# A hybrid decoder trunk in split fp32r products: the first layer's scores as three fp32r products of split queries and keys, and its attention two steps later

## The reference

```
for i in range(DEPTH):                       # DEPTH = 2, x is (1, 256, 2048) float32
    h = rmsnorm(x, g[0])
    y = swa_sink_attention(...) if i == 0 else forgetting_attention(...)
    x = x + rmsnorm(y, g[1]);  h = rmsnorm(x, g[2])
    x = x + rmsnorm((silu(h @ w_gate) * (h @ w_up)) @ w_down, g[3])

swa_sink_attention (32 query heads of 64, 8 key heads, blocks of 128 queries):
    qkv = h @ w_in;  q, k = partial_rotary(q), partial_rotary(k)
    s = einsum('bnqkgd,bnskd->bnkgqs', q, kband) * 64**-0.5, masked to a window of 128
    m = max(max(s), sink);  p = exp(s - m);  probs = p / (sum(p) + exp(sink - m))
    out = (probs @ vband) @ w_out
```

## Time and profile before

| | |
|---|---|
| median of 3 runs | 2123.86 us (2123.24 to 2123.88) |
| profiled execution, its own time | 2122.76 us |
| its span, first to last instruction | 2120.7 us |
| granted TensorE clock, mean | 0.999 of full speed |
| PE / DVE / ACT busy | 99% / 75% / 55% |

### The profile page before, as it was taken

One profiled execution on the slowest core, in us unless ns is written; L12 is line 12 of the kernel. 1 busy time (PEld: TensorE's weight loads), 2 busy tenths in 40 slices (PEclk: granted clock), 3 DMA queues, 4 the chain that ended last, 5 costly groups with the idle time before them and its releaser, 6 DMA issues.

```text
span 2120.7 us, 32295 instructions
## 1 busy us (share of the span) xinstructions
PE 2108.9 (99%) x9723; PEld 1727.9 (81%) x9723; DVE 1598.4 (75%) x3267; ACT 1165.7 (55%) x2093; POOL 151.5 (7%) x291
## 2 busy tenths in 40 slices
PE   9999999999999999999999999999999999999998
PEld 7877888888888888888778777888888888888886
DVE  6777577876678876778888888578776678776786
ACT  7767565544545444555656556565454555445453
POOL 2111000000000000000152241000000000000000
PEclk9999999999999999999999999999999999999999
DMA  7544856565665656665687786656655665656652
GB/s 262 188 140 134 213 180 216 190 188 177 201 214 186 195 171 199 198 199 163 185 249 212 216 234 201 201 191 201 196 180 178 198 217 188 188 177 201 214 188 90
DMA packets 208957, 409.29 MB, mean 193 GB/s; under 512 B 14208, under 2 KB 15392, under 8 KB 208368
## 3 DMA queue, kind: packets, MB, share of 16 engines
q1 hardware_dynamic: 203008, 389.86, 58.8%
q0 software_dynamic: 5584, 18.16, 3.1%
q10 hardware_dynamic: 288, 0.33, 0.0%
HBM read 401.44 MB, written 6.85 MB: 193 GB/s over the span
## 4 chain that ended last, share of the span: by engine, by line
PE 50%; DVE 1%; issue 1%; ACT 0%; POOLq 0%; POOL 0%; DVEq 0%
PE bank L1309 16%; PE bank L1310 16%; PE bank L1311 16%; PE bank L1395 1%; PE bank L1358 1%; DVE ring_lo L786 0%; DVE k_t L846 0%; DVE q_t L857 0%; PE bank L1322 0%; PE bank L1369 0%; ACT y_sb L599 0%; PE bank L1341 0%; POOLq L157 0%; POOL post_r L1168 0%; DVE x_sb L1137 0%
## 5 line engine op out<-in xcount | busy, mean ns | idle before, releaser
L1309 PE MATMUL bank<-ring_hi,a_hi 128*128 128x512 f32 x2240 | 883.1, 394 | 1.0 <-DVE ring_lo L786 1.0
L1311 PE MATMUL bank<-ring_hi,a_lo 128*128 128x512 f32 x2240 | 872.7, 390 | 0.0
L1310 PE MATMUL bank<-ring_lo,a_hi 128*128 128x512 f32 x2240 | 872.4, 389 | 0.0
L586 ACT ACTIVATE ring_hi<-stage,g_t 128x512 fp32r<-128x512 f32 x992 | 661.5, 717 | 363.0 <-DMA stage<-ffn_w_gate_up 207.6
L786 DVE SCALAR_TENSOR_TENSOR ring_lo<-stage,g_t,ring_hi 128x512 fp32r<-128x512 f32 x992 | 707.7, 757 | 162.4 <-ACT ring_hi L586 160.4
L1309 PEld LDWEIGHTS bank<-ring_hi,a_hi 128*128 128x128 f32 x2240 | 420.6, 188 | 91.9 <-issue 5.9
L1311 PEld LDWEIGHTS bank<-ring_hi,a_lo 128*128 128x128 f32 x2240 | 420.5, 188 | 88.8
L1310 PEld LDWEIGHTS bank<-ring_lo,a_hi 128*128 128x128 f32 x2240 | 421.0, 188 | 83.6
L784 DVE TENSOR_TENSOR ring_lo<-stage,ring_hi 128x512 fp32r<-128x512 f32 x480 | 306.9, 690 | 138.1 <-ACT ring_hi L584 136.9
L584 ACT ACTIVATE ring_hi<-stage 128x512 fp32r<-128x512 f32 x480 | 277.8, 624 | 178.3 <-PE bank L1311 154.1
L1309 PE MATMUL bank<-ring_hi,h_hi 128*128 128x512 f32 x704 | 274.4, 390 | 0.0
(11 more groups left out here) (150 smaller groups left out, 861.3 us busy)
## 6 DMA issues: line engine op xcount, KB each, us to landing
stage<-ffn_w_gate_up SPq DMA_DIRECT2D x352, 512.0 KB, 4.6
stage<-ffn_w_down SPq DMA_DIRECT2D x176, 512.0 KB, 5.6
stage<-fox_w_in SPq DMA_DIRECT2D x96, 512.0 KB, 5.0
stage<-swa_w_in SPq DMA_DIRECT2D x48, 512.0 KB, 4.5
stage<-swa_w_out SPq DMA_DIRECT2D x64, 256.0 KB, 4.1
stage<-fox_w_out SPq DMA_DIRECT2D x32, 512.0 KB, 4.8
p_scratch<-p_blocks POOLq DMA_DIRECT2D x12, 384.0 KB, 4.8
p_f<-p_scratch POOLq DMA_DIRECT2D x48, 96.0 KB, 4.6
```

The source lines that it names most:

```text
L586: nc.scalar.activation(ring_hi[:, n % RING, :], src, ACT.Identity, scale=g_t[:, row * KT + j:row * KT + j + 1]).then_inc(hi_ready, 1)
L1309: nc.tensor.matmul(dst, hi_a, hi_w, start=start, stop=False)
L1310: nc.tensor.matmul(dst, hi_a, lo_w, start=False, stop=False)
L1311: return nc.tensor.matmul(dst, lo_a, hi_w, start=False, stop=stop)
```

## The change

The transposed queries and keys of the first layer are split. ACT writes the high part (`high_transposed`, semaphore `qk_high`), DVE then the rest in place of its copy, and only that gives the bank back (`tr_read`). The scores are three fp32r products. All keys of `STD` and `LAST` grow by 2, as do `QK_ATTENDED` (22 to 24) and two entries of `LATE_O`. The second layer is as it was.

```diff
-STD = dict(scores={6: (0, 1), 22: (2, 3)},
-           turned={14: 0, 16: 1, 18: 2, 20: 3, 30: 4, 31: 5, 33: 6, 35: 7},
+STD = dict(scores={8: (0, 1), 24: (2, 3)},
+           turned={16: 0, 18: 1, 20: 2, 22: 3, 32: 4, 33: 5, 35: 6, 37: 7},
...
-QK_ATTENDED = 22
+QK_ATTENDED = 24
...
+            def high_transposed(u, t):
+                act.wait_ge(tr_done, TR[("qk", u, t)] + 1)
+                dst = k_hi if u == 0 else q_hi
+                nc.scalar.activation(dst[:, :, tok(t)], turn_bank(u, t)[:, :].rearrange("p (k m) -> p k m", k=GH // 2),
+                                     ACT.Identity).then_inc(qk_high, 1)
...
             def read_transposed(u, i, t):
-                dve.wait_ge(tr_done, n + 1 + TR_LOOP * i)
-                dst = k_t if u == 0 else q_t
-                nc.vector.tensor_copy(dst[:, :, tok(t)], turn_bank(u, t)[:, :].rearrange("p (k m) -> p k m", k=GH // 2)).then_inc(tr_read, 1)
+                if u < U_FOX:
+                    dve.wait_ge(qk_high, n + 1)
+                    hi, lo = (k_hi, k_lo) if u == 0 else (q_hi, q_lo)
+                    nc.vector.tensor_tensor(lo[:, :, tok(t)], src, hi[:, :, tok(t)].bitcast(F32), ALU.subtract).then_inc(tr_read, 1)
...
                 for lo, hi, keys in ((0, P, P), (P, SEQ, SEQ)):
                     for a in range(2):
+                        if G < NG:
+                            nc.tensor.matmul(dst, q_hi[rows, m, lo:hi], k_hi[rows, b, 0:keys], start=True, stop=False)
...
+                    if G < NG:
+                        for q, k in ((q_hi, k_lo), (q_lo, k_hi)):
+                            for a in range(2):
+                                last = nc.tensor.matmul(score_bank(G, 2 * m + a)[:, lo:lo + keys], q[rows, m, lo:hi], k[rows, b, 0:keys],
+                                                        start=False, stop=k is k_hi)
```

More of the change, by code:

```diff
@@ L54 @@
 U_END = U_FFN[1] + 3 * FG
-STD = dict(scores={6: (0, 1), 22: (2, 3)},
-           maxima={6: (0, 1), 8: (2, 3), 22: (4, 5), 24: (6, 7)},
-           exps={7: 0, 8: 1, 10: 2, 11: 3, 23: 4, 24: 5, 26: 6, 27: 7},
-           scaled={9: 0, 13: 1, 25: 2, 29: 3},
-           turned={14: 0, 16: 1, 18: 2, 20: 3, 30: 4, 31: 5, 33: 6, 35: 7},
[L66 to L72, removed]
+STD = dict(scores={8: (0, 1), 24: (2, 3)},
+           maxima={8: (0, 1), 10: (2, 3), 24: (4, 5), 26: (6, 7)},
+           exps={9: 0, 10: 1, 12: 2, 13: 3, 25: 4, 26: 5, 28: 6, 29: 7},
+           scaled={11: 0, 15: 1, 27: 2, 31: 3},
+           turned={16: 0, 18: 1, 20: 2, 22: 3, 32: 4, 33: 5, 35: 6, 37: 7},
+           pv={24: (0, 1), 40: (2, 3)}, out={25: 0, 41: 1})
+LAST = dict(scores={8: (0, 1), 26: (2,), 33: (3,)},
+            maxima={8: (0, 1), 10: (2, 3), 26: (4, 5), 33: (6, 7)},
+            exps={9: 0, 10: 1, 12: 2, 13: 3, 27: 4, 28: 5, 34: 6, 35: 7},
+            scaled={12: 0, 16: 1, 30: 2, 37: 3},
+            turned={17: 0, 19: 1, 21: 2, 23: 3, 33: 4, 35: 5, 40: 6, 42: 7},
+            pv={26: (0, 1), 45: (2, 3)}, out={})
 FOX = dict(scores={14: (0, 1), 34: (2, 3)},
@@ L114 @@
 LATE_O = {0: [(0, 1)], 2: [(1, 1)], 4: [(2, 1)], 8: [(3, 1)], 10: [(4, 1)], 12: [(5, 0), (5, 1)],
-          26: [(6, 0), (6, 1)], 44: [(7, 0), (7, 1)]}
+          28: [(6, 0), (6, 1)], 46: [(7, 0), (7, 1)]}
 LATE_O_FOX = {0: [(0, 1)], 2: [(1, 1)], 4: [(2, 1)], 6: [(3, 1)], 8: [(4, 1)], 10: [(5, 0), (5, 1)],
@@ L209, in build @@
         q_t = at("q_t", 28 * KB, [P, GH // 2, SEQ])
+        k_hi = at("k_hi", 24 * KB, [P, GH // 2, SEQ], F32R)
+        q_hi = at("q_hi", 28 * KB, [P, GH // 2, SEQ], F32R)
+        k_lo = at("k_lo", 12 * KB, [P, GH // 2, SEQ], F32R)
+        q_lo = at("q_lo", 45 * KB, [P, GH // 2, SEQ], F32R)
         prob = at("prob", 32 * KB, [P, 4, 3 * P + NT])
@@ L252, in build @@
         tr_done, tr_read, qk_turned = sem("tr_done"), sem("tr_read"), sem("qk_turned")
+        qk_high = sem("qk_high")
         scored, row_maxed, maxed, exped = sem("scored"), sem("row_maxed"), sem("maxed"), sem("exped")
@@ L699, in unit @@
                             forget_gate(s + STEPS * (u - U_FOX))
+                        if u < U_FOX:
+                            for v, t in qk_copied(u, s):
+                                high_transposed(v, t)
                     for G, when, at_step in groups(u, s):
@@ L834, in read_transposed @@
                 n = TR[("qk", u, t)]
-                dve.wait_ge(tr_done, n + 1 + TR_LOOP * i)
-                dst = k_t if u == 0 else q_t
-                nc.vector.tensor_copy(dst[:, :, tok(t)], turn_bank(u, t)[:, :].rearrange("p (k m) -> p k m", k=GH // 2)).then_inc(tr_read, 1)
+                src = turn_bank(u, t)[:, :].rearrange("p (k m) -> p k m", k=GH // 2)
+                if u < U_FOX:
+                    dve.wait_ge(qk_high, n + 1)
+                    hi, lo = (k_hi, k_lo) if u == 0 else (q_hi, q_lo)
+                    nc.vector.tensor_tensor(lo[:, :, tok(t)], src, hi[:, :, tok(t)].bitcast(F32), ALU.subtract).then_inc(tr_read, 1)
+                else:
+                    dve.wait_ge(tr_done, n + 1 + TR_LOOP * i)
+                    nc.vector.tensor_copy(q_t[:, :, tok(t)], src).then_inc(tr_read, 1)
             def turn_keys(u, i, a):
@@ L1357, in scores @@
                         rows = slice(DH * a, DH * (a + 1))
-                        last = nc.tensor.matmul(score_bank(G, 2 * m + a)[:, lo:lo + keys], q_t[rows, m, lo:hi], k_t[rows, b, 0:keys], start=True, stop=True)
-                        if lo:
-                            last.then_inc(scored, 1)
+                        dst = score_bank(G, 2 * m + a)[:, lo:lo + keys]
+                        if G < NG:
+                            nc.tensor.matmul(dst, q_hi[rows, m, lo:hi], k_hi[rows, b, 0:keys], start=True, stop=False)
+                        else:
+                            last = nc.tensor.matmul(dst, q_t[rows, m, lo:hi], k_t[rows, b, 0:keys], start=True, stop=True)
+                            if lo:
+                                last.then_inc(scored, 1)
+                    if G < NG:
+                        for q, k in ((q_hi, k_lo), (q_lo, k_hi)):
+                            for a in range(2):
+                                rows = slice(DH * a, DH * (a + 1))
+                                last = nc.tensor.matmul(score_bank(G, 2 * m + a)[:, lo:lo + keys], q[rows, m, lo:hi], k[rows, b, 0:keys],
+                                                        start=False, stop=k is k_hi)
+                                if lo and k is k_hi:
+                                    last.then_inc(scored, 1)
             def transpose_p(G, i, j):
```

## The result

| | before | after |
|---|---|---|
| median of 7 runs | 2123.29 us (2123.12 to 2123.88) | 2130.47 us (2129.7 to 2130.74) |
| ratio to before | 1 | 1.0033, 95% interval 1.0024 to 1.0042 |
| profiled execution | 2122.76 us, span 2120.7 us | 2130.65 us, span 2128.5 us |

The time lies in the range (2123.8 to 2133.5 us) and outside the forecast's own (2125.5 to 2128.5 us). 0.33% is more than the 0.2% that a measurement can tell from no change: the kernel is slower, where "the same" had been the likeliest. That the time lies in the wide range is luck: its upper end was drawn for rival 1, which did not come true, and no term of the prediction stands for the 4 us that were missing.

The account below looks back on a forecast made before the run. TensorE, busy 99%, was taken as the bound. Profiled 2122.76 us + 2.6 (waits at step 5) + 0.3 (scores) = 2125.7 us, plus 1.1 us to the median: 2126.8 us, "the same"; range 2123.8 to 2133.5 us, its own 2125.5 to 2128.5 us.

Parts of the forecast that it names:

- rival 1: Score products: narrow fp32r ones run at the float32 rate, 0.22 us each, 5.3 us more, 2132.1 us; chance 0.20.
- The bound: Whole kernel: TensorE, busy 99%, sets the end; other engines' work costs nothing unless TensorE needs its result too early.
- The scores: Score products on TensorE: a pair takes 0.68 us against 0.66 us, 0.3 us more for 16 pairs.
- rival 2: Score products: the array's two halves don't overlap in fp32r, 10.9 us more, 2137.7 us; chance 0.10.
- Rival 3: Score products: only columns count, saving a quarter, 2.6 us, which pays for the waits; 2124.2 us; 0.08 together with rival 4.
- The wait at step 5: Units 4 to 6: last head's transposes wait for high part and rest to free bank 6; 0.87 us each, 2.6 us.
- What stays covered: ScalarE's and VectorE's other added work, including step 24's high part, costs nothing; 0.9 us of cover left at first head's normalisation.
- in its idle 45%: ScalarE: ten high parts of 0.60 us, 6 us, fit into its idle time.
- Rival 4: Step 5: the waits are hidden and only 0.3 us remain, 2124.2 us; 0.08 together with rival 3.
- the signs named for being wrong: TensorE waits for a normalisation or weight tile, or the three waits sum to under 1.5 or over 4 us.
- nowhere else: TensorE's probability transposes start some 0.9 us late at step 5 of units 4 to 6, three times only.
- the distance: On TensorE, from the first scores to the output projection, between the profiles: must grow by 3 us.

Follow-up runs that it names:

- kernel with heads 6 and 7 first: Changed kernel with STD turning heads 6 and 7 at keys 34 and 35 instead of 35 and 37; 2128.72 us, ratio 1.0024.
- kernel with both causes taken away: Changed kernel with VectorE making block 0's high part in units 3 to 5, heads 6 and 7 turned at steps 2 and 3; 2124.7 us.

## Why the prediction was right in part and wrong in its class

- **The bound** was right: the end moved by TensorE's waits and its own work, 7.2 us, with unchanged shares.
- **The scores** were right in mechanism and short by 0.2 us: a pair takes 0.03 us more, not 0.02 us. Rival 1 (0.22 us a narrow product) is refuted by 0.11 us, rival 2 by the couples of "x2". Rival 3 is refuted for 128 columns by the same 0.11 us; for 256 columns there is a gain, but 0.04 us of 0.44 us and not the quarter. Its own sum also kept 0.3 us that it excludes: it gives 2123.9 us, not 2124.2 us.
- On the rule of the Trainium skill, page "TensorE: Matmul & The Clock Gate", section "Back-to-back issue gap" (some 81 ns for 128 columns): the trace again has 110 ns where each matmul has 128 fresh weight columns. The same page's section "LDWEIGHTS (loading the stationary operand)" gives a load of 128 columns as their number divided by 1.2 in ns, 107 ns: its pace for the load fits the 110 ns. The records of the loads are longer, 0.14 us for the transposes and 0.18 to 0.19 us for these products, and overlap with matmuls. That the weights set the pace was not tested by a run of its own.
- **The wait at step 5** was right in place, count and cause, and 0.10 us a place too small. ScalarE and VectorE were on time to 0.01 us (0.03 us between the two, 0.60 and 0.69 us long). The mis-sized piece is what follows: TensorE started 0.15 us behind VectorE's end at 115.46 us, not 0.05 us as in the earlier trace rows, a row where VectorE made the operand and did not give back the bank. The kernel with heads 6 and 7 first, whose list has no such wait, confirms the cause.
- **The step that failed is "What stays covered"**, where it says of step 24: "the high part stands before the exponentials on ScalarE, and all that follows on VectorE comes 0.63 us later". It then followed VectorE's chain alone, to the normalisation and its 0.9 us of spare time. That part held in units 4 and 5 (head 4's normalisation was done near 107.5 us, TensorE asked at 108.37 us) and failed in unit 6, where TensorE stood 0.41 us for it. The larger part is that the high part waits for TensorE, and ScalarE, being in order, lets ready exponentials stand: they started 2.25 us behind their maxima instead of 0.04 us. The chain on ScalarE (exponentials, projection's read, copy of head 4) ends at TensorE too, and it was not followed. It had 1.10 us of idle time in front of that copy, and none after, with the copy too late by 1.1 us (head 4 was turned by 108.86 us and its copy began at 109.99 us). These waits, at head 5 in three units and at head 4 in unit 6, are the 4 us that were missing; 3.1 us came back when VectorE made the high part.
- The sentence that ScalarE's six further microseconds lie "in its idle 45%" is the same error: the share is right (55% still), and says nothing of one stretch of 6 us without a gap.
- **Rival 4** is refuted: the waits at step 5 aren't hidden.
- **What came true was none of the four rivals.** Of the signs named for being wrong, the three waits at step 5 stayed in their bounds (2.9 us), but "nowhere else" did not hold, the distance grew by 7.3 us and not by 3 us, and TensorE did wait for a normalisation once, in unit 6. The waits for head 5, the greater part, are for ScalarE's copy, which the paragraph doesn't name.

## What to carry to other kernels

When an operation is put into an in-order engine's queue ahead of others, ask when its operand is ready and not only how long it takes: an operation of 0.60 us cost about 4 us in three units, because work that was ready stood behind it for 2.25 us each time, 1.76 us of them idle. Follow every engine's chain from there to the next place where the bottleneck asks for it, and compare the spare time at that place, not the share of busy time. Where the profile names a releaser that had ended long before, read the instruction's other waits in the code; here that led from VectorE to ScalarE, and one edit took the wait away. Look at each place by itself: in unit 6 the same name was right.

## What was new of the hardware

- fp32r matmuls in half of the array's rows run as couples, 3 to 4 ns apart, at 0.11 us for 128 columns and 0.12 us for 256. A float32 matmul there is two recorded passes of 0.11 us for 128 columns and of 0.22 us for 256. So one fp32r product costs half of a float32 one at 128 columns and about a quarter at 256, and three cost more at 128 (0.29 against 0.22 us) and a little less at 256 (0.40 against 0.44 us): together 1.57 against 1.51 us for two pairs.
- The same reading of a bank into fp32r takes 0.60 us on ScalarE (L640) and 0.69 us on VectorE (row of the kernel with both causes taken away):

```profile
102.97 0.69 DVE L856 CAST q_hi<-bank 128x512 fp32r<-128x512 f32 x1 [0.19 <-PE bank L1365]
```

  The slower engine was the better place (3.1 us less in all), since VectorE had time when the operand came and its next work did not stand before TensorE's need.
- TensorE went on 0.14 to 0.15 us behind the VectorE operation that freed the bank, at the two places read here, and 0.05 us behind the one that made its operand; why they differ was not tested. The whole cost of such a wait was its idle time and some 0.16 us of lost overlap.
